# Even front of a two-layer encoder: the backward direction's turn tables are made on GpSimd instead of VectorE

## The reference

```python
for d in range(2):
    lam = lax.complex(jnp.minimum(lam_re[d], -1e-4), lam_im[d])
    dt = jnp.exp(log_dt[d])[:, None]
    lam_bar = jnp.exp(lam * dt)
    b_bar = ((lam_bar - 1.0) / lam)[..., None] * b
    bu = jnp.einsum('blgc,gpc->blgp', ug, b_bar)
    xs = _diag_scan(lam_bar, bu, reverse=(d == 1))      # x_t = lam_bar * x_(t-1) + bu_t
    y = y + jnp.real(jnp.einsum('blgp,gcp->blgc', xs, c)).reshape(bsz, L, W)
```

## Time and profile before

| | |
|---|---|
| median of 3 runs | 3277.49 us (3275.44 to 3277.54) |
| the profiled execution: its own time | 3277.4 us |
| its span, first to last instruction | 3275.8 us |
| TensorE / VectorE / ScalarE / GpSimd busy in the span | 3193.1 / 1664.7 / 1420.4 / 634.7 us |
| granted TensorE clock, mean | 0.992 |
| the 16 batches of the S5 branch | from about 150 us to about 655 us |

### The profile page before, as it was taken

How to read it: one execution, slowest core, us unless ns; L and a number is a source line. 1 busy time by engine, 2 the same in 40 slices (tenths; PEclk the granted TensorE clock), 3 DMA queues, 4 the chain that set the end, 5 groups by cost and what they waited for, 6 DMA issues and landing times. The chain is left out here.

```text
span 3275.8 us, 44209 instructions
## 1 busy us (share of the span) xinstructions
PE 3193.1 (97%) x16472; PEld 2667.7 (81%) x16472; DVE 1664.7 (51%) x3137; ACT 1420.4 (43%) x2568; POOL 634.7 (19%) x450
## 2 busy tenths in 40 slices
PE   7999999999899999999999999999999999999999
PEld 6887888878788888788788888888788888887887
DVE  4899999848766666511413233233322524676211
ACT  5233233243666666500325645455555325664100
POOL 4111111122411110032231011110112112331321
PEclk9999999999999999999999999999999999999999
DMA  4333333276412111643333232322322355445531
GB/s 129 91 98 93 96 97 100 84 220 219 129 43 57 41 47 40 186 118 103 123 91 107 89 121 77 115 89 81 111 81 89 115 190 162 135 140 183 160 102 53
DMA packets 414916, 360.79 MB, mean 110 GB/s; under 512 B 68472, under 2 KB 350584, under 8 KB 414704
## 3 DMA queue, kind: packets, MB, share of 16 engines
q1 hardware_dynamic: 329696, 264.35, 27.9%
q10 hardware_dynamic: 85008, 93.61, 8.2%
HBM read 231.01 MB, written 126.86 MB: 109 GB/s over the span
## 5 line engine op out<-in xcount | busy, mean ns | idle before, releaser
L2883 ACT ACTIVATE eow_w1raw<-of_ring 128x512 f32<-128x512 f32 x218 | 126.7, 596 | 398.0 <-PE of_ring L3284 395.2
L922 PE MATMUL ef_ring<-ef_hhi,ef_whi 128*128 128x512 f32 x664 | 262.8, 396 | 2.2 <-issue 1.0
L923 PE MATMUL ef_ring<-ef_hlo,ef_whi 128*128 128x512 f32 x664 | 259.3, 390 | 0.0
L924 PE MATMUL ef_ring<-ef_hhi,ef_wlo 128*128 128x512 f32 x664 | 259.3, 390 | 0.0
L3110 DVE SCALAR_TENSOR_TENSOR of_state<-of_state,of_small,of_tv 128x256 f32<-128x256 f32 x64 | 56.2, 879 | 240.1 <-ACT of_tv L2945 238.0
L2796 POOL TENSOR_TENSOR eo_w0lo<-of_wraw,eo_w0hi 128x1024 fp32r<-128x1024 f32 x27 | 66.5, 2463 | 452.0 <-ACT eo_w0hi L2837 452.0
L922 PEld LDWEIGHTS ef_ring<-ef_hhi,ef_whi 128*128 128x128 f32 x664 | 125.1, 188 | 33.3 <-issue 7.0
L543 ACT ACTIVATE ef_stage<-ef_ring 128x512 f32<-128x512 f32 x83 | 49.6, 597 | 231.0 <-PE ef_ring L924 230.9
L2796 POOL TENSOR_TENSOR eo_whi<-of_wraw,eo_whi 128x1024 fp32r<-128x1024 f32 x26 | 64.9, 2498 | 432.2 <-ACT eo_whi L2837 432.2
L924 PEld LDWEIGHTS ef_ring<-ef_hhi,ef_wlo 128*128 128x128 f32 x664 | 125.0, 188 | 26.5
L923 PEld LDWEIGHTS ef_ring<-ef_hlo,ef_whi 128*128 128x128 f32 x664 | 125.1, 188 | 24.8
(11 more groups left out here) (683 smaller groups left out, 9390.1 us busy)
## 6 DMA issues: line engine op xcount, KB each, us to landing
of_wraw<-o_w_in SPq DMA_DIRECT2D x53, 512.0 KB, 3.8
ef_wraw<-e_w_in SPq DMA_DIRECT2D x29, 512.0 KB, 4.2
s_tmo<-eow_w1raw ACTq DMA_DIRECT2D x48, 256.0 KB, 2.3
ow_raw<-s_yt SPq DMA_DIRECT2D x18, 512.0 KB, 5.6
ow_raw<-o_w_out SPq DMA_DIRECT2D x16, 512.0 KB, 5.6
s_uc<-ef_stage ACTq DMA_DIRECT2D x24, 256.0 KB, 2.6
ef_ut<-s_uc SPq DMA_DIRECT2D x16, 384.0 KB, 3.3
s_za<-ef_stage ACTq DMA_DIRECT2D x24, 256.0 KB, 2.2
```

What stands on the lines that cost most here:

```text
L922: pe.matmul(out, ah, hhi[:, f, tc], start=(f == 0), stop=False)
L923: pe.matmul(out, ah, hlo[:, f, tc], start=False, stop=False)
L924: mm = pe.matmul(out, al, hhi[:, f, tc], start=False, stop=(f == KT - 1))
L2883: act.activation(stage[i % 4][:, :], ring[i % 3][:, :] if i else start.first, func, scale=GK ** -0.5 if name == "q" else 1.0).then_inc(eva ...
```

## The change

The backward direction's turns (dr = 1) leave VectorE's `turns(b)` and become GpSimd's `turns_back(b)`, which stands right behind `decay(b)` and has its own temporary `back` (128 x 2 x 256) and its own semaphores. ScalarE's `turn_copy` waits for both engines. GpSimd sets `rho` to zero once more ahead of the first batch.

```diff
+        back = s.sb("back", [P, 2, 2 * NCS])
...
+                def turns_back(b):
+                    if b:
+                        pool.wait_ge(hs_done, 2 * b)
+                    q = slice(NPAIR + 2 * b, NPAIR + 2 * b + 2)
+                    a = [bc(ua[x][:, :, q].rearrange("p k j -> p j k"), 3, 2 * CH) for x in range(2)]
+                    e = [bc(ub[x][:, 0:2 * CH, q].rearrange("p k j -> p j k"), 2, CH) for x in range(2)]
+                    out = [tn[:, x, 1, :, 0:NCS] for x in range(2)]
...
+                    for o, x, y in ((o4[0], 0, 0), (o4[1], 0, 1), (t4[0], 1, 1), (t4[1], 1, 0)):
+                        pool.tensor_tensor(o, a[x], e[y], ALU.mult).then_inc(back_mul, 1)
+                    for x, op in ((0, ALU.subtract), (1, ALU.add)):
+                        pool.wait_ge(back_mul, 4 * b + 3 + x)
+                        pool.tensor_tensor(out[x], out[x], tmp[x], op).then_inc(back_add, 1)
+                    pool.wait_ge(back_add, 2 * b + 2)
+                    pool.memset(tn[:, 0, 1, :, 0:1], 0.0).then_inc(back_done, 1)
...
                     if n == LEAD - 3:
                         pool.wait_ge(tab_done, 1)
+                        pool.memset(rho[:, :, :, :], 0.0).then_inc(z_set, 1)
+                        pool.wait_ge(z_set, 5)
                         decay(0)
+                        turns_back(0)
                     if b >= 1 and (n - LEAD) % PER == 1 and b < NB:
                         decay(b)
+                        turns_back(b)
...
-                    act.wait_ge(tn_done, 2 * (b + 1))
+                    act.wait_ge(tn_done, b + 1)
+                    act.wait_ge(back_done, b + 1)
...
-                    for dr in range(2):
-                        at = slice(NCP, NC) if dr == 0 else slice(0, NCS)
...
-                        if dr:
-                            dve.wait_ge(tn_add, 4 * b + 2)
-                        for o, x, y in ((o4[0], 0, 0), (o4[1], 0, 1), (t4[0], 1, 1), (t4[1], 1, 0)):
-                            tt(o, a[x], e[y], ALU.mult).then_inc(tn_mul, 1)
...
+                    out = [tn[:, x, 0, :, NCP:NC] for x in range(2)]
...
+                    for o, x, y in ((o4[0], 0, 0), (o4[1], 0, 1), (t4[0], 1, 1), (t4[1], 1, 0)):
+                        tt(o, a[x], e[y], ALU.mult).then_inc(tn_mul, 1)
...
+                    dve.wait_ge(tn_add, 2 * b + 2)
+                    dve.memset(tn[:, 0, 0, :, NCP:NCP + 1], 0.0).then_inc(tn_done, 1)
```

More of the change, by code:

```diff
@@ L307, in even_front @@
             s.sem(x) for x in ("bt_mm", "btr_done", "lag_mm", "row_copy", "mid_done", "row_done", "lag_out", "v_mm", "rot_mul", "rot_done"))
+        back_mul, back_add, back_done = (s.sem(x) for x in ("back_mul", "back_add", "back_done"))
         rho_done, scan_done, po_mul, hs_done, y_mm = (s.sem(x) for x in ("rho_done", "scan_done", "po_mul", "hs_done", "y_mm"))
@@ L436, in decay @@
                                              ).then_inc(rho_done, 1)
+                def turns_back(b):
[5 more added lines that the diff above has]
+                    out = [tn[:, x, 1, :, 0:NCS] for x in range(2)]
+                    o4 = [x.rearrange("p j (a b) -> p j a b", b=2 * CH) for x in out]
+                    tmp = [back[:, x, :].rearrange("p (j n) -> p j n", j=2) for x in range(2)]
+                    t4 = [x.rearrange("p j (a b) -> p j a b", b=2 * CH) for x in tmp]
+                    if b:
+                        pool.wait_ge(back_add, 2 * b)
+                    for o, x, y in ((o4[0], 0, 0), (o4[1], 0, 1), (t4[0], 1, 1), (t4[1], 1, 0)):
[5 more added lines that the diff above has]
+                    pool.memset(tn[:, 0, 1, :, 0:1], 0.0).then_inc(back_done, 1)
                 pool.memset(warm[:, :], 1.0).then_inc(warm_set, 1)
@@ L756, in inputs @@
                         dve.wait_ge(bp_done, 2 * b)
-                        dve.wait_ge(tn_add, 4 * b)
+                        dve.wait_ge(tn_add, 2 * b)
                     pk_ = [bc(pwb[x][:, b, :, :].rearrange("p t q -> p q t"), 3, GC) for x in range(2)]
@@ L789, in turns @@
                         dve.wait_ge(hs_done, 2 * b)
-                    for dr in range(2):
-                        at = slice(NCP, NC) if dr == 0 else slice(0, NCS)
[L792 to L798, removed]
-                        if dr:
-                            dve.wait_ge(tn_add, 4 * b + 2)
-                        for o, x, y in ((o4[0], 0, 0), (o4[1], 0, 1), (t4[0], 1, 1), (t4[1], 1, 0)):
-                            tt(o, a[x], e[y], ALU.mult).then_inc(tn_mul, 1)
-                        for x, op in ((0, ALU.subtract), (1, ALU.add)):
-                            dve.wait_ge(tn_mul, 8 * b + 4 * dr + 3 + x)
-                            tt(out[x], out[x], tmp[x], op).then_inc(tn_add, 1)
@@ L806, in turns @@
-                    for dr, c0 in ((0, NCP), (1, 0)):
-                        dve.wait_ge(tn_add, 4 * b + 2 * dr + 2)
-                        dve.memset(tn[:, 0, dr, :, c0:c0 + 1], 0.0).then_inc(tn_done, 1)
+                    q = slice(2 * b, 2 * b + 2)
+                    a = [bc(ua[x][:, :, q].rearrange("p k j -> p j k"), 3, 2 * CH) for x in range(2)]
+                    e = [bc(ub[x][:, 0:2 * CH, q].rearrange("p k j -> p j k"), 2, CH) for x in range(2)]
+                    out = [tn[:, x, 0, :, NCP:NC] for x in range(2)]
@@ new lines, in turns @@
+                    o4 = [x.rearrange("p j (a b) -> p j a b", b=2 * CH) for x in out]
+                    tmp = [tt_[x][:, 0:2 * NCS].rearrange("p (j n) -> p j n", j=2) for x in range(2)]
+                    t4 = [x.rearrange("p j (a b) -> p j a b", b=2 * CH) for x in tmp]
+                    for o, x, y in ((o4[0], 0, 0), (o4[1], 0, 1), (t4[0], 1, 1), (t4[1], 1, 0)):
+                        tt(o, a[x], e[y], ALU.mult).then_inc(tn_mul, 1)
+                    for x, op in ((0, ALU.subtract), (1, ALU.add)):
+                        dve.wait_ge(tn_mul, 4 * b + 3 + x)
+                        tt(out[x], out[x], tmp[x], op).then_inc(tn_add, 1)
```

## The result

The changed kernel takes 3282.88 us (median of 16 runs, 3281.48 to 3286.51); the kernel before takes 3276.39 us beside it (16 runs, 3270.15 to 3279.51). The ratio is 1.0022, interval 1.0015 to 1.0030: slower by 0.22%, about 7 us. The forecast was slower by 0.35%, 3288.9 us, in a range of 3277 to 3306. Times are medians; one run of e7 took 5848.84 us at a granted clock of 0.789 and is left out.

A forecast was written before the change was run, and what follows sets the result against it. VectorE was taken to bound the even front: 3.74 us of holds less 2.92 saved is 0.82 us a batch, times 14 is 11.5, on 3277.4 gives 3288.9 us. Range 3277 to 3306, the forecast's own 3284 to 3297.

The forecast's parts named there:

- What bounds the kernel: Even front: VectorE sets the pace at 31.2 us a batch; TensorE needs 30.14 and stands ready some 0.7 us.
- The hold on VectorE: In the turns, GpSimd's six SBUF-reading instructions hold up VectorE's two-SBUF-input instructions, 3.74 us a batch against 2.92 saved.
- the two places of the trace: Ahead of the first batch and behind the last, GpSimd seemed to hold VectorE for its own length less 0.20 us.
- A draw: Rival: GpSimd's turns hold VectorE 0.49 to 0.57 us each, net 0 to 0.47 us a batch, within 6.6 us; chance 0.14.
- The turns of the first and the last batch are free: Batch 0 hides ahead of VectorE's wait, batch 15 in TensorE's 6.8 us lateness; only 14 batches pay 0.82 us.
- The tables are in time: Ahead of rotate: ScalarE's copies end at 9.3 us behind hs_done, VectorE arrives at 11.8, cover 2.5 us.
- Held for the whole length: Rival: GpSimd's turns hold VectorE for all their recorded time, 4.94 us a batch, 28.3 us, 3305.7 us; chance 0.15.
- The short read: Rival: turns hold VectorE as little as decay's copies, 0.9 us a batch; TensorE bounds, 3267.7 us; chance 0.11.
- The late tables: Rival: GpSimd's turns take 2 us each, so rotate waits 3 us a batch, some 40 us in all; chance 0.04.
- The clock: Rival: longer TensorE waits could lower its granted clock, as to 0.83 once before; taken as part of the range.
- The signs: L860 to rotate about 11.8 us, VectorE products 1.1 to 1.3, GpSimd rows about 1.2, TensorE's chunk_out waits some 21.
- What a relief of VectorE would be worth: Even front: taking work from VectorE gains at most 9.7 us, TensorE's summed waits, as TensorE is the next bound.

The follow-up runs named there:

- e7: Kernel before the change, one more GpSimd wait so decay's copies stand beside the first rotate instead of unrotate: 3268.3 us against 3277.1, ratio 0.9973.
- e2: Changed kernel with each of GpSimd's four products made twice, ten instructions a batch: 3312.4 us, ratio 1.0108 to the kernel before.
- e6: Changed kernel with four more plain GpSimd sums a batch into a temporary nothing reads: 3310.9 us, ratio 1.0101 to the kernel before.
- e1: Changed kernel with GpSimd's six turn instructions made memsets, backward turns left out: 3259.9 us against 3276.0 for the kernel before, ratio 0.9950.
- e4: Changed kernel with only the four products on GpSimd, behind decay; subtraction and addition on VectorE: 3279.45 us against 3276.0 for the kernel before, ratio 1.0011.
- e5: Changed kernel with only the four products on GpSimd, started beside VectorE's scans; sums on VectorE: 3280.5 us against 3277.1 for the kernel before, ratio 1.0011.
- e3: Changed kernel with only the four products on GpSimd, one batch ahead beside the rotates; sums on VectorE: 3262.72 us against 3276.0 before, ratio 0.9958.

## Why the prediction was right, and where its sizes were off

**What bounds the kernel** was right: VectorE sets the pace in the batches. The added net cost of 14 batches came out on the sixteenth `chunk_out` undiminished (7.7 us), and e2 and e6 grew with the number of instructions.

**The hold on VectorE** was right in kind: e1 shows that it takes a GpSimd instruction that reads SBUF, e4 and e5 that a VectorE instruction with both inputs there is held, a scan too, and e3 and e7 that the rotate, with one input in PSUM, isn't. That it is the place of the input, and not another trait of the rotate, is argued: no run moved that input alone.

**Its size was the term that was off.** I took 3.74 us a batch and measured 0.55 + 2.92 = 3.47 us (7.68 us in 14 batches, and the 2.92 saved), 0.58 us for each of six on the average: 0.59 for a product, 0.56 for a sum. The products were priced at 0.67 us from L467, which is 0.87 us long at the shortest; the turns' products are 0.78 us by themselves (the first batch, where VectorE idles, and e3). Length less 0.20 us, the rule that I had from the two places of the trace, gives 0.58 for them. I applied it to the wrong row. The 1.27 us of the earlier trace rows was also the longer of the distances there: the two before it are 1.06 and 1.08 us (starts at 678.97, 680.03 and 681.11 us), which would have priced L467 at under 0.5 us, so the 0.20 us was less firm than "both places agree" says. The sums I took at 0.53, slightly too low. The error of 0.27 us a batch is 3.8 us, all of the distance between 11.5 and 7.7.

**How near it was.** The measured time lies in the wide range but just below the forecast's own of 3284 to 3297 us. Of the 6.0 us between 3288.9 and 3282.9, 3.8 are the price, 1.0 is the kernel before, which measured 3276.4 and not 3277.4, and the rest is the drift behind the even front, which nothing explains. The net of 0.55 us a batch is also only 0.08 us above the top of the rival *A draw* (0.47), and 0.22% is hardly over the 0.2% that I said could be told from no change. The profiles separate the two better than the time does: both executions start `chunk_out` at the same time in the first batch and 7.7 us apart in the fifteenth.

**The turns of the first and the last batch are free**: right. The first `chunk_out` stands where it stood, and behind the fifteenth all moved as one.

**The tables are in time**: right. ScalarE's two copies start at 415.33 and 415.66 us and VectorE's rotate starts at 419.31 with the same 0.20 us ahead of it as before.

**The rivals.** Held for the whole length (28 us) is out: 0.59 of 0.78 us. The short read is out for products and sums, though it is what the copies of `decay` do. The late tables didn't occur. The clock fell twice in the changed kernel's even front, to 0.89 from 247 to 262 us behind a wait of 2.66 us and to 0.83 from 310 to 320 us behind one of 1.84 us, where it fell once before. Neither cost time: the next `chunk_out` started 0.1 us behind the end of `unrotate` both times (279.83 behind 279.72 us, 345.56 behind 345.45), as in a batch at 1.00.

**The signs.** From L860's like to the rotate VectorE takes 419.31 - 407.81 = 11.50 us, where I said 11.8 and it was 10.97. The products and GpSimd's rows are as long as I said, but the first `inputs` kept its length: GpSimd's six instructions end with VectorE's own half of the turns. TensorE's waits ahead of `chunk_out` are 14.6 us and not 21, for the reason that follows.

**What a relief of VectorE would be worth** was wrong. I said 9.7 us at the most, the sum of TensorE's wait rows, and e3 took 14.6 us off the same stretch. The rows count less than stands still. Two starts of `chunk_out` of the kernel before, 30.67 us apart, have a wait of 0.26 us between them:

```profile
435.33 1.54 PE L982 MATMUL ef_tq<-ef_ut,ef_wt 128*128 128x192 f32 x8 [0.52 <-issue]
...
466.00 1.54 PE L982 MATMUL ef_tq<-ef_ut,ef_wt 128*128 128x192 f32 x8 [0.26 <-issue]
```

A batch needs 30.14 us, so 0.53 us were lost and half of it was shown. A matmul of 512 columns is drawn 0.39 us long but is followed after 0.23 us, which hides 0.16 us of each wait; the instructions behind a wait start slower (1.54 against 1.46 us for the eight). Eleven such waits make 3 us. Most of the rest is the stretch at the clock of 0.83, which I had set at little: from 342.51 to 374.37 us a batch took TensorE 31.86 us with no wait at its end, 1.72 us over the 30.14, and ten microseconds at 0.83 are 1.7 short of full clock. In e1 and e3, where no `chunk_out` waits, the clock is 1.00 in the whole stretch. That last share was not tried by itself.

## What to carry to other kernels

Before work goes from VectorE to GpSimd, look at what VectorE runs beside it: where both read SBUF with two inputs on VectorE's side, each GpSimd instruction took its own length less about 0.2 us out of VectorE's queue here (less about 0.3 beside the 128x512 instructions), and at 0.58 us for 0.35 to 0.53 saved the move loses. The same products placed where VectorE reads PSUM, or waits anyway, were free here; with the sums left on VectorE the kernel was 0.4% faster than the kernel before and 0.6% faster than the changed one. How far the next engine is behind is read from the distance of its starts in batches with and without a wait, not from the sum of its wait rows.

## What the runs showed that I had not expected

The four small copies of `decay`, there all along, cost 0.58 us a batch beside `unrotate` and nothing that the rows show beside the rotate; one wait more on GpSimd made the kernel before 0.27% faster (e7). In e5 a GpSimd product took 2.24 us beside the scans, nearly three times its length: the loss falls on both engines.
